# Cached sequences of layer one: other places and another order for the loads of their keys and values

## The chip, the core and the metric

The kernel runs on one core of a Trainium2 chip. A time is device microseconds (us) of one execution of the whole program on that core. Engines are named as in the profile: PE is TensorE (matrix products and transposes), PEld its weight loads, DVE is VectorE, ACT is ScalarE, POOL is GpSimd, SP is SyncE, which in this kernel only issues DMAs. Each engine runs its own list of instructions in order and waits on semaphores that the others, or landed DMAs, raise.

## The reference

One step of a two-layer trunk, for a prompt of 512 tokens and for 8 sampled sequences of 16 new tokens each, every one of them with 256 cached tokens. What matters here is layer one for the sampled sequences:

```
q, k, v, g = split(h @ w_in_a)                     # 16 heads of 64
k_all, v_all = concat(cache_k, k), concat(cache_v, v)   # 256 cached + 16 new rows
z = q @ k_all.T / 8
a = exp(log_sigmoid(z) + sum of log_sigmoid(-z) over later keys)   # stick-breaking
o = a @ v_all
y = (o * silu(g)) @ w_out_a;  x = x + gate * rmsnorm(y)
```

So each sequence reads its own 1 MB of cached keys (256 x 1024 in 32-bit floats), 1 MB of cached values, and its 16 new value rows (64 KB), which the kernel itself has written to an output shortly before. Layer two does the like with another attention.

## The kernel before

Large products (projections, the gate's columns) are made in three passes over operands split into a high and a low part; they stand at lines 1671 to 1673 and fill most of the span. All tiles lie in one arena in on-chip memory, cut into regions by hand: X, RA, RB, RC, RD, KN of 20 KB a partition each, WR of 16 and RH of 5. A name is a view of a place there, and one place has several names over time. The order of the work is written out by hand for every engine, in the blocks `sync` (SP), `gpsimd`, `scalar`, `vector` and `tensor`; nothing schedules it later.

The stretch around the change has three parts.

The pairs (from about 230 to 370 us): the prompt's attention, two heads at a time, eight pairs, PE's `pair_a`, with the gate's projection in its gaps. SP loads the gate's weights meanwhile (`gates`, L575) and, at two fixed places, `early_a` the keys of sequences 0 and 1 (`load_k`, L588). The last product of a pair is `values_a` (L1860); it reads the prompt's values in RC, which is free for other things only when the last of them is done.

The cached sequences (370 to 424 us): PE's `sample_a(s, ...)` runs once for each of the 8 sequences. Its order for sequence s is: transpose the keys of sequence s+1 (`turn_k`, 16 transposes, L1899), transpose the result of sequence s-1 (`turn_o`, L1934), transpose the weights of sequence s (L1947), scores of sequence s+1 (L1920, L1926), and last the product of weights and values of sequence s (48 small products, L1962). ACT makes the sigmoids, DVE the running products, both copy what PE has transposed. Keys come into two places `kc[0]`, `kc[1]`, values into `vc[0]`, `vc[1]`, new rows into `vnew[0]`, `vnew[1]`, by the sequence's parity.

SP's list sets when each of these loads starts. `next_k(s)` waits until the keys of sequence s-2 have been transposed (semaphore `c_k_transposed`), then issues two DMAs of 512 KB. `load_v(s)` waits until the product of sequence s-2 is done (`c_o_ready`), then issues two DMAs of 512 KB and one of 64 KB for the new rows. SP takes them strictly in turn, so a DMA that stands behind a wait can't start before that wait is over, whatever it needs itself. Before the change the list is: keys 2, keys 3, values 2, keys 4, values 3, keys 5, and so on, the middle part as a loop in which places come from registers.

The output projection (`project` with the name ya, from 428 us): its weights come in eight loads (`load(n)`, L523) through two places `wraw[0]`, `wraw[1]`. The first two are issued at about 350 us, in the pairs. ACT splits the first (`w_high`, L779) between the sequences 6 and 7.

The lines that the text speaks of:

```
def next_k(s, b):                            # before: SP
    sp.wait_ge(c_kt, s * 4 + (HEAD - 4))     # keys s-2 transposed
    load_k(s, b)
def load_v(s, b):
    sp.wait_ge(c_av, s + (HEAD - 1))         # product s-2 done
    ...                                      # two DMAs of values, one of new rows
```

Of the kernel before, what the change touches and what calls it, by code (L numbers as in the profile page):

```python
# [28 lines left out]
P = 128  # L29
D = 1024  # L30
# [3 lines left out]
NSEQ = 8  # L34
NEW = 16
# [3 lines left out]
PK = PAST // P  # L39
# [3 lines left out]
NC = 512  # L43
# [7 lines left out]
HEAD = 8  # L51
# [45 lines left out]
def build(nc, i, o):  # L97
    ctx = ExitStack()
    with ctx:
# [3 lines left out]
        def sem(name):  # L103
            return ctx.enter_context(nc.semaphore(name))
# [7 lines left out]
        def region(kb):  # L112
            a = arena[:, at[0] * KB:(at[0] + kb) * KB]
            at[0] += kb
            return a

        X, RA, RB, RC, RD, KN = (region(20) for _ in range(6))
        X_r, RA_r = (rounded[:, 20 * KB * n:20 * KB * (n + 1)] for n in range(2))
        WR, RH = region(16), region(5)
# [7 lines left out]
        def sub(r, a, n):  # L127
            return r[:, int(a * KB):int(a * KB) + n]

        def cut(r, a, /, **dims):  # L130

            names = " ".join(dims)
            return sub(r, a, math.prod(dims.values())).rearrange(f"p ({names}) -> p {names}", **dims)
# [57 lines left out]
        def halves(r, k):  # L191
            return r[:, k:k + 4, 0:SEQ].rearrange("p (k c) n -> p k c n", c=2)

        kc = [cut(WR, 8, k=PK, c=2, n=NC), halves(kT, 0)]
        vc = [halves(kT, 4), cut(KN, 0, k=PK, c=2, n=NC)]
        vnew = [sub(KN, 16, D), sub(RC, 16, D)]
        ktc = [cut(X, 8.5 * b, k=PAIRS, n=KEYS) for b in range(2)]
        qb = cut(X, 17, k=PAIRS, n=32)
        so = cut(RH, 3, b=2, n=2 * P)
        sbeta, sstay, sex = (cut(RC, 2.25 * b, g=2, n=KEYS) for b in range(3))  # L200
        sAT = cut(RH, 0, g=2, k=3, n=P)

        kcb = [cut(WR, 8 * b, k=PK, c=2, n=NC) for b in range(2)]

# [12 lines left out]
        caches = {  # L217
            "ak": i["cache_a_k"].rearrange("a s (k p) (c h) d -> (a s) p k c (h d)", p=P, c=2),
            "av": i["cache_a_v"].rearrange("a s (k p) (c h) d -> (a s) p k c (h d)", p=P, c=2),
            "bk": i["cache_b_k"].rearrange("s (k p) (a h) c d -> s p k a (h c d)", p=P, a=2),  # L220
            "bv": i["cache_b_v"].rearrange("s (k p) (c h) d -> s p k c (h d)", p=P, c=2),
        }
# [30 lines left out]
        SL = 4  # L253
        A0, YA, B0, YB = 0, 6, 8, 14
# [14 lines left out]
        tasks, task_end = [], []  # L269
# [44 lines left out]
        def batch_buffer(m):  # L314
# [12 lines left out]
        s_mu, s_macc, s_msum, s_mout, s_mdone = (sem(n) for n in (  # L327
            "mod_slot_used", "mod_first_summed", "mod_partial_read", "mod_out", "mod_read"))
# [20 lines left out]
        c_kt, c_krA, c_krV, c_q, c_z, c_sig, c_ex, c_mul, c_t, c_at, c_av, c_or, c_ot, c_od = (sem("c_" + n) for n in (  # L349
            "k_transposed", "k_read_act", "k_read_dve", "q_staged", "z_ready", "sigmoids", "scanned",  # L350
            "a_ready", "t_ready", "at_ready", "o_ready", "o_read", "o_transposed", "o_done"))
        c_k, c_v, c_vn = ([sem(f"c_{n}_in{b}") for b in range(2)] for n in ("k", "v", "vnew"))

        b_s, b_mx, b_nb, b_p, b_rc, b_c1, b_w, b_t, b_wt, b_o, b_or = (sem("b_" + n) for n in (
# [151 lines left out]
        def _(sp):  # L506
# [12 lines left out]
            def load(n):  # L519
                ci, s = divmod(n, SL)  # L520
                if n >= 2:
                    sp.wait_ge(s_wlo, n - 1)
                sp.dma_start(wraw[n % 2].rearrange("p (k n) -> p k n", k=2), piece(chunks[ci][1], chunks[ci][2], s))\  # L523
                    .then_inc(s_w[n % 2], 16)
# [61 lines left out]
            def load_k(s, b):  # L586
                for k in range(PK):
                    sp.dma_start(kc[b][:, k], caches["ak"][s, :, k]).then_inc(c_k[b], 16)  # L588

            def next_k(s, b):  # L590
                sp.wait_ge(c_kt, s * 4 + (HEAD - 4))
                load_k(s, b)

            def load_v(s, b):
                sp.wait_ge(c_av, s + (HEAD - 1))
                for k in range(PK):
                    sp.dma_start(vc[b][:, k], caches["av"][s, :, k]).then_inc(c_v[b], 16)
                sp.dma_start(vnew[b][0:NEW, :], av_rows[s]).then_inc(c_vn[b], 16)

            def early_a(p):  # L600

                if p == 2:
                    sp.wait_ge(s_mu, BATCHES)
                    load_k(0, 0)
                elif p == 6:
                    sp.wait_ge(a_z, HEAD + 8 * 4)
                    load_k(1, 1)

            gates(0, SL * YA, early_a)
            sp.wait_ge(s_glo[0], HEAD + PAIRS)  # L610
            load(SL * YA)
            load(SL * YA + 1)
            sp.wait_ge(s_stored["av"], 32)
            sp.wait_ge(a_z, HEAD + 8 * PAIRS)
            load_v(0, 0)
            sp.wait_ge(a_av, HEAD + PAIRS)
            load_v(1, 1)
            next_k(2, 0)
            with sp.Fori(1, NSEQ // 2 - 1) as it:
                for b in range(2):  # L620
                    next_k(it * 2 + (b + 1), 1 - b)
                    load_v(it * 2 + b, b)
            next_k(NSEQ - 1, 1)
            load_v(NSEQ - 2, 0)
            load_v(NSEQ - 1, 1)
            sp.wait_ge(c_z, HEAD + 2 * NSEQ)
            sp.dma_start(x[:, 0:NT, :], i["x_prompt"].rearrange("b (t p) n -> p (b t) n", p=P)).then_inc(s_xr, 16)
            sp.dma_start(x[:, NT, :], i["x_sample"].rearrange("s q n -> (s q) n")).then_inc(s_xr, 16)
# [1029 lines left out]
        def _(pe):  # L1658
# [278 lines left out]
            def sample_a(s, b, more, first=False):  # L1937
                if more:
                    turn_k(kc, turned, bank_a, read_a, c_k, PK, c_kt, s + 1)
                if not first:  # L1940
                    turn_o(s - 1, 1 - b)
                for g in range(2):
                    pe.wait_ge(c_mul, s * 2 + (HEAD + g + 1))
                    pe.wait_ge(c_at, s * 2 + (HEAD + g - 1))
                    for k in range(3):
                        w = P if k < 2 else NEW
                        last = tp(ps[4 + g][0:w, P * k:P * (k + 1)], sbeta[:, g, P * k:P * k + w], ident)  # L1947
                    last.then_inc(c_t, 1)
                if more:
                    scores_s(s + 1, ktc, 1 - b, qb, (c_krA, c_krV), c_q, c_z, c_sig, True)  # L1950
                pe.wait_ge(c_v[b], (s - b) * 16 + 32)
                pe.wait_ge(c_vn[b], (s - b) * 8 + 16)
                pe.wait_ge(c_or, s + HEAD)
                for k in range(3):
                    w = P if k < 2 else NEW
                    for g in range(2):
                        if k == 0:
                            pe.wait_ge(c_at, s * 2 + (HEAD + g + 1))
                        for j in range(4):
                            pair = slice(P * (4 * g + j), P * (4 * g + j + 1))  # L1960
                            v_ = vc[b][:, k, g, P * j:P * (j + 1)] if k < 2 else vnew[b][0:NEW, pair]
                            last = mm(ps[6][32 * j:32 * j + 32, P * g:P * (g + 1)], sAT[0:w, g, k, 32 * j:32 * j + 32], v_,  # L1962
                                      start=k == 0 and g == 0, stop=k == 2, skip_group_check=True)
                last.then_inc(c_av, 1)
# [154 lines left out]
```

## Time and profile before

| | |
|---|---|
| median of 3 runs (lowest, highest) | 928.01 us (926.48, 928.21) |
| the profiled execution, its whole time | 926.95 us |
| its span, first to last instruction | 925.2 us |
| PE busy, share of the span | 878.4 us, 95% |
| PEld, DVE, ACT, POOL | 74%, 52%, 44%, 3% |
| granted PE clock, mean | 0.994 |
| DMA, mean over the span | 150 GB/s |

The profiled execution is one run of the program; its time is 1.06 us under the median of the three. Times within the profile count from the first instruction. The granted clock is 1.00 at 2.4 GHz and 0.50 at 1.2 GHz.

### The profile page before, as it was taken

What the parts mean: (1) busy time and instruction counts of PE and PEld (TensorE: products, weight loads), DVE (VectorE), ACT (ScalarE), POOL (GpSimd) and SP (SyncE); (2) the same over time, 40 slices, a digit from 0 to 9 for tenths busy, and PEclk for the clock granted to TensorE, in tenths of its full rate; (3) what the DMA queues carried; (4) which work ended last, traced back from release to release, by engine and by line L of the source; (5) the groups of instructions that cost most, each with busy time, mean ns of one, the idle gap of its engine ahead of it and who ended that gap; (6) DMA issues with size and microseconds to landing.
All of it is one profiled execution on the core that took longest, in us unless ns stands there. A gap on an engine that the chain in (4) does not pass through costs nothing.

```text
span 925.2 us, 15133 instructions
## 1 busy us (share of the span) xinstructions
PE 878.4 (95%) x5814; PEld 683.8 (74%) x5814; DVE 477.1 (52%) x888; ACT 408.9 (44%) x891; POOL 29.8 (3%) x79
## 2 busy tenths in 40 slices
PE   5899999999999999997999799999989999998897
PEld 4677667777777778675888688888867888776685
DVE  4442334222487776567347524342376565477835
ACT  5341221212466665567245412342246666567622
POOL 0000000000000000110000000000000000022000
PEclk9999999999999999998999999999999999999999
DMA  9955645774510202795233224343211030387522
GB/s 306 369 211 217 229 157 185 288 270 144 204 48 24 92 1 95 269 322 182 72 110 114 68 70 154 97 142 120 80 69 46 23 95 2 139 305 277 187 93 114
DMA packets 72914, 138.57 MB, mean 150 GB/s; under 512 B 4368, under 2 KB 31376, under 8 KB 72720
## 3 DMA queue, kind: packets, MB, share of 16 engines
q1 hardware_dynamic: 69360, 126.60, 39.7%
q0 software_dynamic: 3200, 11.01, 3.2%
q8 instruction: 47, 0.77, 0.3%
q14 instruction: 19, 0.16, 0.1%
q10 hardware_dynamic: 288, 0.04, 0.0%
HBM read 121.38 MB, written 16.25 MB: 149 GB/s over the span
## 4 chain that ended last, share of the span: by engine, by line
PE 83%; DVE 6%; ACT 5%; issue 3%; DMA 2%; SPq 1%; ACTq 0%; DVEq 0%
PE bank L1671 20%; PE bank L1673 19%; PE bank L1672 19%; PE bank L1745 3%; PE bank L1721 2%; PE bank L1841 2%; PE bank L1995 2%; PE bank L1860 2%; PE bank L1852 2%; PE bank L2011 2%; DMA arena<-in_mod_w_a 1%; PE bank L1920 1%; PE bank L1899 1%; PE bank L2004 1%; PE bank L2052 1%
## 5 line engine op out<-in xcount | busy, mean ns | idle before, releaser
L1671 PE MATMUL bank<-w_parts,h_parts 128*128 128x512 f32 x640 | 258.0, 403 | 10.5 <-DVE h_parts L1206 6.1
L1673 PE MATMUL bank<-w_parts,h_parts 128*128 128x512 f32 x640 | 251.2, 392 | 0.0
L1672 PE MATMUL bank<-w_parts,h_parts 128*128 128x512 f32 x640 | 250.8, 392 | 0.0
L1671 PEld LDWEIGHTS bank<-w_parts,h_parts 128*128 128x128 f32 x640 | 121.1, 189 | 44.1 <-issue 15.5
L779 ACT ACTIVATE w_parts<-arena 128x1024 fp32r<-128x1024 f32 x64 | 67.4, 1054 | 179.9 <-PE bank L1673 166.6
L1200 DVE TENSOR_TENSOR w_parts<-arena,w_parts 128x1024 fp32r<-128x1024 f32 x64 | 78.2, 1223 | 129.3 <-ACT w_parts L779 128.8
L1673 PEld LDWEIGHTS bank<-w_parts,h_parts 128*128 128x128 f32 x640 | 121.0, 189 | 26.5
L1672 PEld LDWEIGHTS bank<-w_parts,h_parts 128*128 128x128 f32 x640 | 121.4, 190 | 23.1
L1671 PE MATMUL bank<-h_parts,w_parts 128*128 128x320 f32 x256 | 89.5, 350 | 1.6 <-ACT arena L896 0.9
L1673 PE MATMUL bank<-h_parts,w_parts 128*128 128x320 f32 x256 | 79.2, 309 | 0.0
L1672 PE MATMUL bank<-h_parts,w_parts 128*128 128x320 f32 x256 | 79.0, 309 | 0.0
L1385 DVE TENSOR_TENSOR_SCAN arena<-arena 128x511 f32<-128x511 f32 (+3 forms) x64 | 52.3, 817 | 26.6 <-ACT arena L906 26.6
L1671 PEld LDWEIGHTS bank<-h_parts,w_parts 128*128 128x128 f32 x256 | 48.4, 189 | 3.1 <-issue 1.7
L1672 PEld LDWEIGHTS bank<-h_parts,w_parts 128*128 128x128 f32 x256 | 48.6, 190 | 0.0
L1673 PEld LDWEIGHTS bank<-h_parts,w_parts 128*128 128x128 f32 x256 | 48.0, 188 | 0.0
L1745 PE MATMUL bank<-const,arena 128*128 128x128 f32 x280 | 41.3, 277 | 6.8 <-DVE arena L1375 2.0
L1745 PEld LDWEIGHTS bank<-const,arena 128*128 128x128 f32 x280 | 32.6, 141 | 19.0 <-issue 5.6
L905 ACT ACTIVATE arena<-bank 128x512 f32<-128x512 f32 (+3 forms) x64 | 28.4, 443 | 38.8 <-PE bank L1852 37.8
L828 ACT ACTIVATE arena<-bank 128x512 f32<-128x512 f32 x36 | 21.5, 598 | 54.1 <-PE bank L1673 53.9
L1206 DVE TENSOR_TENSOR h_parts<-arena,h_parts 128x640 fp32r<-128x640 f32 (+1 forms) x40 | 31.2, 793 | 26.6 <-ACT h_parts L784 26.5
L784 ACT ACTIVATE h_parts<-arena 128x640 fp32r<-128x640 f32 (+1 forms) x40 | 28.0, 714 | 25.2 <-PE bank L1673 14.2
L835 ACT ACTIVATE arena<-bank 128x512 f32<-128x512 f32 x21 | 12.5, 596 | 56.1 <-PE bank L1745 56.0
(170 smaller groups left out, 1183.1 us busy)
## 6 DMA issues: line engine op xcount, KB each, us to landing
arena<-in_w_in_a SPq DMA_DIRECT2D x32, 512.0 KB, 4.0
arena<-in_mod_w_b SPq DMA_DIRECT2D x12, 1024.0 KB, 6.6
arena<-in_mod_w_a SPq DMA_DIRECT2D x10, 1024.0 KB, 10.2
arena<-in_mod_w_kv SPq DMA_DIRECT2D x8, 1024.0 KB, 6.3
arena<-in_cache_a_k SPq DMA_DIRECT2D x16, 512.0 KB, 6.1
arena<-in_cache_a_v SPq DMA_DIRECT2D x16, 512.0 KB, 4.9
arena<-in_w_kv_b SPq DMA_DIRECT2D x16, 512.0 KB, 3.8
arena<-in_w_in_b SPq DMA_DIRECT2D x16, 512.0 KB, 3.9
```

The costliest lines, as they stand in the source:

```text
L779: nc.scalar.activation(whl[:, n % 2, 0, :], wraw[n % 2], ACT.Copy).then_inc(s_whi, 1)
L784: nc.scalar.activation(hhi[:, k, n], h_src[name][:, k, n], ACT.Copy).then_inc(s_hhi, 1)
L828: nc.scalar.activation(dst_of[kind][:, t, NC * (c % 2):NC * (c % 2 + 1)], ps[t][:, :], ACT.Copy).then_inc(s_pjA, 1)
L905: nc.scalar.activation(beta[:, u % 4, 0:w], ps[u % 4][:, 0:w], ACT.Sigmoid, scale=SCALE)
L1200: nc.vector.tensor_tensor(whl[:, n % 2, 1, :], wraw[n % 2], whl[:, n % 2, 0, :].bitcast(F32), ALU.subtract)\
L1206: nc.vector.tensor_tensor(hlo[:, k, n], h_src[name][:, k, n], hhi[:, k, n].bitcast(F32), ALU.subtract)\
L1385: nc.vector.tensor_tensor_scan(ex[:, u % 2, 0:w - 1][:, ::-1], st, st, 1.0, ALU.mult, ALU.bypass)\
L1671: mm(out, ah, wh, start=start, stop=False)
L1672: mm(out, ah, wl, start=False, stop=False)
L1673: return mm(out, al, wh, start=False, stop=stop)
L1721: last = mm(ps[5][32 * j:32 * j + 32, :], cT[:, 2 * s + kk, :], batch_buffer(m)[:, kk, NC * b:NC * (b + 1)], start=s == 0, stop=s == SL - ...
L1745: last = tp(ps[uses[n][1]][:, P * b:P * (b + 1)], src[:, t, P * f:P * (f + 1)], ident)
```

## The change

Sequence 0 gets two places of its own for its values, `vfirst` (4 KB each at KN 16 and RH 0), loaded in the pairs at the third step of `gates`, right behind the keys of sequence 0, under a semaphore of its own (`c_v_first_in`). `vc[0]` is therefore free at the end of the pairs, and the values of sequence 2 go there, where the values of sequence 0 went. Both places for new rows now lie in RC (RC 12 and RC 16), so the new rows of sequence 0 are loaded behind the last `values_a`. `so` and `sAT` move from RH to RC. The first output weights are loaded between product 5 and the values of sequence 7, the second ones behind the new rows of sequence 7. SP's loop is written out, and its list reads: keys s, wait for product s-2, values s (from s = 3), new rows s, then the same for s+1.

```diff
--- before.py
+++ after.py
@@ -193,12 +193,13 @@
 
         kc = [cut(WR, 8, k=PK, c=2, n=NC), halves(kT, 0)]
         vc = [halves(kT, 4), cut(KN, 0, k=PK, c=2, n=NC)]
-        vnew = [sub(KN, 16, D), sub(RC, 16, D)]
+        vfirst = [cut(r, a, c=2, n=NC) for r, a in ((KN, 16), (RH, 0))]
+        vnew = [sub(RC, 12, D), sub(RC, 16, D)]
         ktc = [cut(X, 8.5 * b, k=PAIRS, n=KEYS) for b in range(2)]
         qb = cut(X, 17, k=PAIRS, n=32)
-        so = cut(RH, 3, b=2, n=2 * P)
+        so = cut(RC, 10, b=2, n=2 * P)
         sbeta, sstay, sex = (cut(RC, 2.25 * b, g=2, n=KEYS) for b in range(3))
-        sAT = cut(RH, 0, g=2, k=3, n=P)
+        sAT = cut(RC, 7, g=2, k=3, n=P)
 
         kcb = [cut(WR, 8 * b, k=PK, c=2, n=NC) for b in range(2)]
 
@@ -349,6 +350,7 @@
         c_kt, c_krA, c_krV, c_q, c_z, c_sig, c_ex, c_mul, c_t, c_at, c_av, c_or, c_ot, c_od = (sem("c_" + n) for n in (
             "k_transposed", "k_read_act", "k_read_dve", "q_staged", "z_ready", "sigmoids", "scanned",
             "a_ready", "t_ready", "at_ready", "o_ready", "o_read", "o_transposed", "o_done"))
+        c_v0 = sem("c_v_first_in")
         c_k, c_v, c_vn = ([sem(f"c_{n}_in{b}") for b in range(2)] for n in ("k", "v", "vnew"))
 
         b_s, b_mx, b_nb, b_p, b_rc, b_c1, b_w, b_t, b_wt, b_o, b_or = (sem("b_" + n) for n in (
@@ -592,9 +594,10 @@
                 load_k(s, b)
 
             def load_v(s, b):
-                sp.wait_ge(c_av, s + (HEAD - 1))
                 for k in range(PK):
                     sp.dma_start(vc[b][:, k], caches["av"][s, :, k]).then_inc(c_v[b], 16)
+
+            def load_new(s, b):
                 sp.dma_start(vnew[b][0:NEW, :], av_rows[s]).then_inc(c_vn[b], 16)
 
             def early_a(p):
@@ -602,27 +605,31 @@
                 if p == 2:
                     sp.wait_ge(s_mu, BATCHES)
                     load_k(0, 0)
+                    sp.wait_ge(s_mdone, len(tasks))
+                    for k in range(PK):
+                        sp.dma_start(vfirst[k], caches["av"][0, :, k]).then_inc(c_v0, 16)
                 elif p == 6:
                     sp.wait_ge(a_z, HEAD + 8 * 4)
                     load_k(1, 1)
 
             gates(0, SL * YA, early_a)
             sp.wait_ge(s_glo[0], HEAD + PAIRS)
-            load(SL * YA)
-            load(SL * YA + 1)
             sp.wait_ge(s_stored["av"], 32)
             sp.wait_ge(a_z, HEAD + 8 * PAIRS)
-            load_v(0, 0)
+            load_v(2, 0)
             sp.wait_ge(a_av, HEAD + PAIRS)
+            load_new(0, 0)
             load_v(1, 1)
-            next_k(2, 0)
-            with sp.Fori(1, NSEQ // 2 - 1) as it:
-                for b in range(2):
-                    next_k(it * 2 + (b + 1), 1 - b)
-                    load_v(it * 2 + b, b)
-            next_k(NSEQ - 1, 1)
-            load_v(NSEQ - 2, 0)
-            load_v(NSEQ - 1, 1)
+            load_new(1, 1)
+            for s in range(2, NSEQ):
+                next_k(s, s % 2)
+                sp.wait_ge(c_av, s + (HEAD - 1))
+                if s == NSEQ - 1:
+                    load(SL * YA)
+                if s > 2:
+                    load_v(s, s % 2)
+                load_new(s, s % 2)
+            load(SL * YA + 1)
             sp.wait_ge(c_z, HEAD + 2 * NSEQ)
             sp.dma_start(x[:, 0:NT, :], i["x_prompt"].rearrange("b (t p) n -> p (b t) n", p=P)).then_inc(s_xr, 16)
             sp.dma_start(x[:, NT, :], i["x_sample"].rearrange("s q n -> (s q) n")).then_inc(s_xr, 16)
@@ -1948,7 +1955,10 @@
                     last.then_inc(c_t, 1)
                 if more:
                     scores_s(s + 1, ktc, 1 - b, qb, (c_krA, c_krV), c_q, c_z, c_sig, True)
-                pe.wait_ge(c_v[b], (s - b) * 16 + 32)
+                if s == 0:
+                    pe.wait_ge(c_v0, 32)
+                else:
+                    pe.wait_ge(c_v[b], (s - b) * 16 + 32 * b)
                 pe.wait_ge(c_vn[b], (s - b) * 8 + 16)
                 pe.wait_ge(c_or, s + HEAD)
                 for k in range(3):
@@ -1958,7 +1968,8 @@
                             pe.wait_ge(c_at, s * 2 + (HEAD + g + 1))
                         for j in range(4):
                             pair = slice(P * (4 * g + j), P * (4 * g + j + 1))
-                            v_ = vc[b][:, k, g, P * j:P * (j + 1)] if k < 2 else vnew[b][0:NEW, pair]
+                            old = vfirst[k % 2] if s == 0 else vc[b][:, k % 2]
+                            v_ = old[:, g, P * j:P * (j + 1)] if k < 2 else vnew[b][0:NEW, pair]
                             last = mm(ps[6][32 * j:32 * j + 32, P * g:P * (g + 1)], sAT[0:w, g, k, 32 * j:32 * j + 32], v_,
                                       start=k == 0 and g == 0, stop=k == 2, skip_group_check=True)
                 last.then_inc(c_av, 1)
```

Two pieces of SP's list follow, each before and after. The first is the start of the sequences. The names are: `in_cache_a_v` cached values, `in_cache_a_k` cached keys (128x1024 goes to the even place, 128x2x512 to the odd one), `out_av_s` the new rows. Before, from the new rows of sequence 1 on, up to the values of sequence 2:

```order
L598 DMA arena<-out_av_s 16x1024
L588 DMA arena<-in_cache_a_k 128x1024 [waits c_k_transposed]
L588 DMA arena<-in_cache_a_k 128x1024
L619 UNCONDITIONAL_BRANCH
L619 ISA
L588 ISA [waits c_k_transposed]
L588 DMA arena<-in_cache_a_k 128x2x512
L588 ISA
L588 DMA arena<-in_cache_a_k 128x2x512
L595 REGISTER_ALU
L597 ISA [waits c_o_ready]
L597 DMA arena<-in_cache_a_v 128x2x512
```

Keys 2 and keys 3 stand one behind the other, ahead of the first wait for a product. After the change, SP's list from the new rows of sequence 0 on, up to the keys of sequence 4:

```order
L601 DMA arena<-out_av_s 16x1024 [waits a_o_ready]
L598 DMA arena<-in_cache_a_v 128x1024 x2
L601 DMA arena<-out_av_s 16x1024
L590 DMA arena<-in_cache_a_k 128x1024 [waits c_k_transposed]
L590 DMA arena<-in_cache_a_k 128x1024
L601 DMA arena<-out_av_s 16x1024 [waits c_o_ready]
L590 DMA arena<-in_cache_a_k 128x2x512 [waits c_k_transposed]
L590 DMA arena<-in_cache_a_k 128x2x512
L598 DMA arena<-in_cache_a_v 128x1024 [waits c_o_ready]
L598 DMA arena<-in_cache_a_v 128x1024
L601 DMA arena<-out_av_s 16x1024
L590 DMA arena<-in_cache_a_k 128x1024 [waits c_k_transposed]
```

Keys 3 moved behind the wait for product 0, and keys 4 behind the wait for product 1 and behind the values and new rows of sequence 3. Keys 5 to 7 stand in the same way behind products 2 to 4.

The second is the end of the sequences on SP, where `in_w_out_a` are the output weights and `in_x_prompt`, `in_x_sample` the residual stream. Before:

```order
L588 DMA arena<-in_cache_a_k 128x2x512 [waits c_k_transposed]
L588 DMA arena<-in_cache_a_k 128x2x512
L597 DMA arena<-in_cache_a_v 128x2x512 [waits c_o_ready]
L597 DMA arena<-in_cache_a_v 128x2x512
L598 DMA arena<-out_av_s 16x1024
L597 DMA arena<-in_cache_a_v 128x1024 [waits c_o_ready]
L597 DMA arena<-in_cache_a_v 128x1024
L598 DMA arena<-out_av_s 16x1024
L627 DMA arena<-in_x_prompt 128x4x1024 [waits c_z_ready]
```

Keys 7, values 6, values 7 and the residual stream follow each other. After the change, from the keys of sequence 7 on:

```order
L590 DMA arena<-in_cache_a_k 128x2x512 [waits c_k_transposed]
L590 DMA arena<-in_cache_a_k 128x2x512
L525 DMA arena<-in_w_out_a 128x2x512 [waits w_low,c_o_ready]
L598 DMA arena<-in_cache_a_v 128x1024 x2
L601 DMA arena<-out_av_s 16x1024
L525 DMA arena<-in_w_out_a 128x2x512 [waits w_low]
L634 DMA arena<-in_x_prompt 128x4x1024 [waits c_z_ready]
```

One load of output weights now stands ahead of the values of sequence 7, one behind its new rows.

## Rows read from the trace of the kernel before

**Rows 1.** The page's slices: DMA's busy tenths, 40 slices of 23.1 us.

```profile
DMA  9955645774510202795233224343211030387522
```

**Rows 2.** Waits on PE from 376 to 417.2 us: total, times, longest.

```profile
PE bank L1899 <- DMA arena<-in_cache_a_k: 0.6, 1, 0.6
```

**Rows 3.** Busy time by stretch: length, engines, then granted clock, DMA share, GB/s.

```profile
376.00:382.60 6.60, 5.29 (x85) 3.42 (x83) 4.07 (x8) 4.18 (x14) 1.93 (x6) 1.00 0.98 354
389.00:395.00 6.00, 5.80 (x95) 4.24 (x92) 4.00 (x9) 3.80 (x11) 1.10 (x4) 1.00 1.00 360
424.80:425.90 1.10, 0.00 (x0) 0.00 (x0) 1.04 (x3) 0.00 (x0) 0.00 (x0) 1.00 1.01 400
```

**Rows 4.** Timeline of PE in the sequences: start, us, line, shapes, idle before.

```profile
380.99 1.65 PE L1962 MATMUL bank<-arena 128*32 128x128 f32 x48
383.22 2.00 PE L1899 MATMUL bank<-const,arena 128*128 128x128 f32 x16 [0.58 <-DMA arena<-in_cache_a_k]
...
388.96 2.00 PE L1899 MATMUL bank<-const,arena 128*128 128x128 f32 x16
...
394.93 2.00 PE L1899 MATMUL bank<-const,arena 128*128 128x128 f32 x16
...
412.88 2.00 PE L1899 MATMUL bank<-const,arena 128*128 128x128 f32 x16
...
421.06 1.76 PE L1962 MATMUL bank<-arena 128*32 128x128 f32 x48 [0.36 <-ACT arena L963]
```

**Rows 5.** Timeline of SP: start of the issue, us taken, line, what.

```profile
363.06 1.20 SPq L597 DMA_DIRECT2D arena<-in_cache_a_v  x2
...
374.41 0.84 SPq L597 DMA_DIRECT2D arena<-in_cache_a_v  x2
375.30 0.43 SPq L598 DMA_DIRECT2D arena<-out_av_s  x1
375.77 3.89 SPq L588 DMA_DIRECT2D arena<-in_cache_a_k  x4
382.84 1.27 SPq L597 DMA_DIRECT2D arena<-in_cache_a_v  x2
...
389.09 0.82 SPq L597 DMA_DIRECT2D arena<-in_cache_a_v  x2
...
392.24 0.54 SPq L588 DMA_DIRECT2D arena<-in_cache_a_k  x1
```

**Rows 6.** The chain of waits at 376 us: start, us, what.

```profile
376.23 6.94 DMA arena<-in_cache_a_k
```

**Rows 7.** Single DMA issues, begun at 374.41, 392.24, 304.10: size, us to landing.

```profile
arena<-in_cache_a_v SPq DMA_DIRECT2D x1, 512.0 KB, 3.7
...
arena<-in_cache_a_k SPq DMA_DIRECT2D x1, 512.0 KB, 6.6
...
arena<-in_cache_a_k SPq DMA_DIRECT2D x1, 512.0 KB, 5.7
```

**Rows 8.** Busy time by stretch, where PE stood still, columns as in rows 3.

```profile
32.70:35.20 2.50, 0.00 (x0) 0.02 (x1) 1.47 (x3) 0.74 (x1) 0.00 (x0) 1.00 1.09 354
524.10:527.00 2.90, 0.00 (x1) 0.00 (x0) 1.23 (x3) 2.54 (x4) 0.00 (x0) 1.00 0.00 0
528.40:531.70 3.30, 3.30 (x9) 2.54 (x8) 0.17 (x1) 0.60 (x1) 0.00 (x0) 0.50 0.89 299
```

**Rows 9.** Timeline of PE, the first products behind those two stops.

```profile
35.21 0.47 PE L1671 MATMUL bank<-w_parts,h_parts 128*128 128x512 f32 x1 [2.56 <-DVE h_parts L1206]
...
527.09 0.50 PE L1671 MATMUL bank<-w_parts,h_parts 128*128 128x512 f32 x1 [2.99 <-DVE w_parts L1200]
```

**Rows 10.** The chain of waits, one product below and one at full clock.

```profile
430.61 0.43 PE bank L1673
...
433.76 0.23 PE bank L1673
```

**Rows 11.** Timeline of ACT: the first output weights are split.

```profile
419.28 1.05 ACT L779 ACTIVATE w_parts<-arena 128x1024 fp32r<-128x1024 f32 x1
```

## The prediction, made before the changed kernel ran

> **What bounds the kernel now.** I read the page's slices first, then the stretch of the cached sequences by busy time, the waits of PE in it, and the timelines of PE and SP side by side.
>
> The slices show DMA's busy share high from slice 16 on (counted from 0), tenths 7 and 9 in the two slices that hold 370 to 416 us [rows 1]. The table by stretch says how high: from 376 to 382.6 us the share is 0.98 at 354 GB/s, and 1.00 at 360 GB/s from 389 to 395 [rows 3]. So the queue is full there. Yet PE hardly waits for it: over the sequences PE's list of waits has one wait on a load, 0.6 us, for the keys of sequence 2 [rows 2]; it ends at 383.22 after 0.58 us of idleness [rows 4]. PE is busy 5.80 of 6.00 us in a normal sequence [rows 3]. What the reader is to see: a full queue that is not a bottleneck, because its loads start early. How early is the thing the change touches.
>
> The period of a normal sequence, start of one key transpose to the next, is 394.93 - 388.96 = 5.97 us; the one whose keys were late took 388.96 - 383.22 = 5.74 from its late start [rows 4]. So a late start gives 0.23 us back within its sequence.
>
> How early do keys start? Keys 2 and 3 are issued from 375.77 in one group of four [rows 5], keys 3 well before product 0 has even begun at 380.99 [rows 4]. Keys 5 end with the issue at 392.24, which takes 6.6 us [rows 5, 7], so they land at 398.84; they are needed one period after 394.93, at 400.9. That leaves two us to spare, because SP reaches keys 5 behind product 1 and not behind product 2.
>
> **The change, part by part.**
>
> Values of sequence 0 leave the head of the queue. Before, they were issued at 363.06 [rows 5], 18 us before their product at 380.99 [rows 4]: hidden, so moving them gives nothing. Their 1 MB in the pairs, at about 242 us, meets a DMA busy share of half at most (slices 10 and 11) [rows 1]; no engine waits there on a load that I can price, cost 0, at most the few hundredths of a gate load that starts later. Values of sequence 2 take their place at 363.06, also 0.
>
> New rows 0 now stand first at 374.41, when the last pair's product is done. They are needed at 380.99. The 512 KB load issued at 374.41 took 3.7 us [rows 7]; 64 KB take no longer, so they land by 378.1: cost 0, cover 2.9 us. But they push values 1, new rows 1 and keys 2 back by one issue, 0.43 us [rows 5]. Keys 2 land at 376.23 + 6.94 = 383.17 before [rows 6] and PE waits for exactly that, so the wait grows from 0.58 to about 1.0: +0.4 us. Bounds: 0 if the short transfer is absorbed in the queue, 0.43 if not; I take 0.4, since the landing of keys 2 was the end of a full row of transfers.
>
> The new order of SP's list is the large term. Keys s+1 now stand behind the wait for product s-2, and from s = 3 behind values s and new rows s. Keys 3: after product 0, SP starts at 382.84 [rows 5], issues new rows 2, then keys 3, the second half at about 383.7. A load of that size into that place took 5.7 us in the pairs [rows 7], so it lands at 389.4; PE wants it at 388.96 + 0.4 = 389.36. Just in time: 0.
>
> Keys 4: SP restarts after product 1, at 389.09 before [rows 5] and 389.49 now, and issues values 3 (two), new rows 3, keys 4 (two). The same five DMAs in the same order, values, new rows, keys, stand in the trace, started from an idle queue at 374.41: the last landed at 383.17, 8.76 us later [rows 5, 6]. So keys 4 land at 398.25, and PE wants them at 394.93 + 0.4 = 395.33. It stops for about 2.95 us; less the 0.23 that a late start gives back, 2.7. Product 3 is then late, but product 2 was not, and the loads behind product 2 bring keys 5 at 404.2, against 404.0 at which PE now arrives: a wait of 0.2, given back. Product 3, late, releases keys 6: late by the same 2.95, net 2.7. Keys 7 are like keys 5. So only every second key load stops PE: 0.4 + 2.7 + 2.7 = 5.8 us. In short, each stop costs the length of the five loads less 6.0 us.
>
> That length is the disputed number. Below: the first 512 KB from an idle queue takes 3.7 us [rows 7], 2.4 of it not transfer if 512 KB move at 400 GB/s, the highest rate of these rows [rows 3]; the five DMAs hold 2112 KB, 5.4 us at that rate: 7.8 us, hence 2 x 1.8 and no term for keys 2, 3.5 us in all. Above: in the full queue values 3 were issued at 389.09 and keys 5 landed at 398.84, 9.75 us [rows 5, 7]: 2 x 3.7 + 0.4 = 7.8 us. I take 8.76, because that row is the same bundle from the same state of the queue.
>
> The Trainium skill, "DMA: Bandwidth & Descriptors", section "Anatomy of one DMA", fits a DMA by about 2.0 us plus bytes over 436 GB/s. Taken for the bundle as one transfer that would be an estimate of 7.0 us, two stops of 0.9, and 2.3 us in all with keys 2. The trace speaks against it: 8.76 us for the same bundle, and 354 to 360 GB/s over whole stretches with the queue full.
>
> What the stops do to the clock. PE stood still for 2.99 us before 527.09, and the granted clock in 528.40 to 531.70 is 0.50, the lower of the two levels; PE stood still for 2.56 us before 35.21 and the clock stayed at 1.00 [rows 8, 9]. My stops of 2.95 us lie close to the first. One such stretch of 3.30 us at half clock loses 3.30 x (1 - 0.23/0.43) = 1.5 us, by the spacing of one product at either level [rows 10]. Transposes and scores are on the chain right behind a late key, so all of it counts. Bounds: 0 and, for both stops, 3.1. I take one: 1.5.
>
> The output weights. The first load now starts after product 5, which by the sum ends at about 418.8; with 3.7 us it lands at 422.5. ACT splits it at 419.28 before [rows 11], now 5.8 later at 425.1: cover 2.6 us, cost 0. Behind it come values 7 and new rows 7; the four DMAs, one half-MB fewer than the bundle, take about 8.8 - 1.5 = 7.3 us from 418.8, so 426.1, and product 7 wants them at 421.06 + 5.8 = 426.9 [rows 4]: 0, with the thinnest cover of all. The second output weights are used a whole weight slot later: 0. The loop written out and the moved places add no instruction to PE, ACT or DVE: 0.
>
> Sum: 926.95 + 5.8 + 1.5 = 934.3 for the profiled execution. That execution is 1.06 under the median of the three, and the changed kernel will be told by its median too, so I forecast 928.0 + 7.3 = 935.3 us.
>
> **Rivals.**
>
> The clock holds. For it: 2.56 us did no harm [rows 9], and the stops could be shorter than 2.95. Against: 2.99 did. Time 928.0 + 5.8 = 933.8.
>
> The bundle is short, 7.8 us. For it: fewer bytes are under way at a time than before, and 400 GB/s occurs. Against: the same bundle took 8.76. Then 928.0 + 3.5 = 931.5, with stops of about 2 us and no fall of the clock. The Trainium skill's fit, "DMA: Bandwidth & Descriptors", section "Anatomy of one DMA", would make it 930.3, as an estimate.
>
> The bundle is long and the clock falls twice. For it: loads in the full queue took 9.75. Against: after each stop the queue has drained. 928.0 + 7.8 + 3.1 = 938.9.
>
> Not slower: the keys come in time. The stretch is bound by bytes, and the change takes a megabyte of values out of the full part, from 382.84 to 363.06; the queue is then emptier wherever keys stand. Price: the wait of 0.58 us goes, of which 0.23 was given back, so -0.4, 927.6. It decides at a bundle of 6.0 us; with 2.4 us that are not transfer, 2112 KB would have to move at 600 GB/s. Or the transposes of keys 4 would have to be released by something earlier than the order shows. I find neither in the rows.
>
> **How the numbers follow.** Late keys with one fall of the clock 0.50, its own range 933.0 to 937.0; clock holds 0.22; short bundle 0.14; long bundle 0.09; not slower 0.05. The range goes from the low bound over the profiled execution, 926.95 + 3.5 = 930.5, to the long bundle's 939.0. A measurement here tells 0.2%, 1.9 us, from no change. Every case but the last is beyond that: slower 0.94. The last one's 0.4 us is within it: 0.04 for the same, and 0.02 for a gain that I have no mechanism for.
>
> **What would show it.** Right: PE's waits at the key transposes of sequences 4 and 6 end with the landing of `in_cache_a_k`, near 3 us each, those of 5 and 7 near 0.2; the wait at sequence 2 is 1.0; SP issues keys 4 at about 390.8 instead of 386; DMA's share in 389 to 416 falls under 0.9, with more idle between bundles; the clock shows 0.50 behind a stop. The chain of waits passes through loads of keys for 15 to 20 us. Wrong: waits at every sequence of the same length (then the queue never drains and the length is that of the full queue); no wait at keys 4 (then the order of SP was misread); a wait at product 7 for values or new rows; or a first output load that ACT waits for.

## The result, and the profile after

The changed kernel takes 937.98 us, the median of 4 runs (936.64 to 939.23), against 928.11 of before (926.48 to 928.69): the ratio is 1.0104, with a 95% interval of 1.0087 to 1.0122. That is 9.9 us slower; 7.3 were forecast, and 938.0 lies inside the stated range. The profiled execution took 939.23 us, the slowest of the four, with a span of 937.4 us, 12.2 over the span before.

PE's timeline at the start of each key transpose, after (start, us taken, line, shapes, idle before it and what ended it); the lines answer to [rows 4]:

```profile
371.48 2.00 PE L1906 MATMUL bank<-const,arena 128*128 128x128 f32 x16
...
384.68 2.00 PE L1906 MATMUL bank<-const,arena 128*128 128x128 f32 x16 [0.62 <-DMA arena<-in_cache_a_k]
...
390.77 2.00 PE L1906 MATMUL bank<-const,arena 128*128 128x128 f32 x16 [0.28 <-DMA arena<-in_cache_a_k]
...
399.67 2.90 PE L1906 MATMUL bank<-const,arena 128*128 128x128 f32 x16 [3.09 <-DMA arena<-in_cache_a_k]
...
406.88 2.00 PE L1906 MATMUL bank<-const,arena 128*128 128x128 f32 x16
...
416.20 2.44 PE L1906 MATMUL bank<-const,arena 128*128 128x128 f32 x16 [3.27 <-DMA arena<-in_cache_a_k]
...
423.38 2.01 PE L1906 MATMUL bank<-const,arena 128*128 128x128 f32 x16
...
432.73 1.65 PE L1973 MATMUL bank<-arena 128*32 128x128 f32 x48 [1.53 <-DMA arena<-out_av_s]
```

The first row is the transpose of keys 0 (keys 1 are left out), then keys 2 to 7, and the last is product 7. PE stops for 3.09 us before keys 4 and for 3.27 before keys 6, both ended by the landing of keys; keys 5 and 7 are not waited for. The start times also show what follows a stop: keys 4 to keys 5 takes 7.21 us and keys 6 to keys 7 takes 7.18, where 5.74 was read from the late sequence of before. The transposes themselves take 2.90 and 2.44 us there, not 2.00.

The waits of PE on loads, from 369 to 445 us (total, times, longest), answer to [rows 2]:

```profile
PE bank L1906 <- DMA arena<-in_cache_a_k: 7.3, 4, 3.3
...
PE bank L1973 <- DMA arena<-out_av_s: 1.5, 1, 1.5
```

0.6 us of waiting has become 8.8. SP's timeline (start of the issue, us taken, line, what), with [rows 5] beside it, shows why:

```profile
375.83 0.35 SPq L601 DMA_DIRECT2D arena<-out_av_s  x1
376.22 0.90 SPq L598 DMA_DIRECT2D arena<-in_cache_a_v  x2
377.16 0.43 SPq L601 DMA_DIRECT2D arena<-out_av_s  x1
377.63 0.90 SPq L590 DMA_DIRECT2D arena<-in_cache_a_k  x2
...
390.55 0.81 SPq L598 DMA_DIRECT2D arena<-in_cache_a_v  x2
391.40 1.51 SPq L601 DMA_DIRECT2D arena<-out_av_s  x1
392.96 0.90 SPq L590 DMA_DIRECT2D arena<-in_cache_a_k  x2
...
407.01 0.82 SPq L598 DMA_DIRECT2D arena<-in_cache_a_v  x2
407.87 0.43 SPq L601 DMA_DIRECT2D arena<-out_av_s  x1
408.34 0.90 SPq L590 DMA_DIRECT2D arena<-in_cache_a_k  x2
```

SP goes on at 390.55, when product 1 is done, and reaches keys 4 at 392.96. And the chain of waits (start, us, what), which before had one load of keys in the sequences [rows 6], now has three:

```profile
378.10 6.54 DMA arena<-in_cache_a_k
393.42 6.20 DMA arena<-in_cache_a_k
408.80 7.35 DMA arena<-in_cache_a_k
```

Keys 4 land at 393.42 + 6.20 = 399.62, which is 9.07 us after SP went on; keys 6 at 416.15, 9.14 us after 407.01. Last, busy time by stretch (length, engines, granted clock, DMA share, GB/s):

```profile
35.40:38.60 3.20, 3.20 (x11) 2.51 (x11) 0.00 (x0) 1.46 (x3) 0.00 (x0) 0.50 1.10 348
400.60:403.90 3.30, 3.30 (x18) 3.10 (x16) 1.87 (x4) 1.19 (x3) 0.00 (x0) 0.50 1.04 338
404.00:417.00 13.00, 9.52 (x165) 6.72 (x164) 6.10 (x12) 6.29 (x21) 2.16 (x6) 1.00 0.68 242
417.70:421.00 3.30, 3.30 (x21) 2.48 (x24) 1.49 (x4) 1.66 (x5) 0.00 (x0) 0.50 1.01 335
```

Behind each of the two stops the clock is at 0.50 for about 3.3 us. DMA's share over the thirteen us between them is 0.68; over 389 to 416 us it is 0.75, where the same stretch of time before has 0.94. The queue idles (from 406 to 407 us it moves no packet) and PE waits for it, by turns.

From these starts the sequences can be booked: the shift of a row against the same row of before is 1.42 us at keys 0, then 1.46 at keys 2, 1.81 at keys 3, 4.74, 5.97, 9.31 and 10.50 at keys 4 to 7, 11.67 at product 7, and 10.80 at the first product of the output projection (438.94 against 428.14). So 9.4 us arise in the sequences. The 1.42 us ahead of them are a stretch at half clock from 35.4 to 38.6 us, behind a stop of PE that left the clock at 1.00 in the profile of before [rows 8, 9]; nothing of the change stands there. The 1.4 us that are left of the 12.2 arise behind the first output product, where the stretches at half clock stand at other places in the two profiles (528.4 us before only, 697.5 and 861.4 us after only).

### The profile page after: what moved, and what is told of

It is laid out like the page before. It is cut to its first block, busy times and chain, and to the rows that moved or that the text cites. A ratio compares the mean times of both kernels' runs of the same rounds, so it can differ in the third digit from the quotient of the medians.

```text
span 937.4 us, 15081 instructions
## 1 busy us (share of the span) xinstructions
PE 885.1 (94%) x5814; PEld 689.4 (74%) x5814; DVE 477.6 (51%) x888; ACT 409.3 (44%) x891; POOL 29.7 (3%) x79
## 4 chain that ended last, share of the span: by engine, by line
PE 83%; DVE 5%; DMA 4%; ACT 4%; issue 2%; SPq 1%; POOL 0%; DVEq 0%; ACTq 0%
PE bank L1678 19%; PE bank L1680 18%; PE bank L1679 18%; PE bank L1752 3%; PE bank L1728 2%; PE bank L1848 2%; PE bank L2006 2%; PE bank L1906 2%; DMA arena<-in_cache_a_k 2%; PE bank L1867 2%; PE bank L1859 2%; PE bank L2022 2%; PE bank L1927 1%; DMA arena<-in_mod_w_a 1%; PE bank L2063 1%
## 5 line engine op out<-in xcount | busy, mean ns | idle before, releaser
L1752 PE MATMUL bank<-const,arena 128*128 128x128 f32 x280 | 41.7, 279 | 7.5 <-DVE arena L1382 2.0
L1752 PEld LDWEIGHTS bank<-const,arena 128*128 128x128 f32 x280 | 32.9, 142 | 20.1 <-issue 6.1
L835 ACT ACTIVATE arena<-bank 128x512 f32<-128x512 f32 x36 | 21.5, 598 | 52.6 <-PE bank L1680 52.4
L1906 PE MATMUL bank<-const,arena 128*128 128x128 f32 x256 | 34.5, 286 | 8.9 <-DMA arena<-in_cache_a_k 7.3
```

What stands on the lines that cost most here:

```text
L835: nc.scalar.activation(dst_of[kind][:, t, NC * (c % 2):NC * (c % 2 + 1)], ps[t][:, :], ACT.Copy).then_inc(s_pjA, 1)
L1752: last = tp(ps[uses[n][1]][:, P * b:P * (b + 1)], src[:, t, P * f:P * (f + 1)], ident)
L1906: last = tp(bank(("k", s, c))[:, PAST * a + P * k:PAST * a + P * (k + 1)], kcs[s % 2][:, k, j // 4, P * (j % 4):P * (j % 4 + 1)], ident)
```

## The experiments

The theory (A): the keys' place in SP's list is the loss, because the load of keys s+1 now starts only when product s-2 is done, behind the values of s; to this comes the clock, which falls behind the stops. Rivals: the moved places and the early first values cost by contention (B); the output weights' loads at the end do (C).

**Keys ahead of the wait again.** The changed kernel with one edit:

```diff
             for s in range(2, NSEQ):
-                next_k(s, s % 2)
+                if s + 1 < NSEQ:
+                    next_k(s + 1, (s + 1) % 2)
                 sp.wait_ge(c_av, s + (HEAD - 1))
```

(with `next_k(2, 0)` ahead of the loop.)

> The changed kernel with one edit: keys s+1 stand ahead of the wait for product s-2 again, as before the change; places, first values, third values and output weights stay as changed. Theory A (the loss is the place of the keys in SP's list): the stops at keys 4 and 6 go, no key wait is over 0.7 us, the time is 927.5 to 929.5. Rival B (the loss is the moved places and the early first values, by contention): stays at 934 or more. Rival C (the loss is the output weights' loads at the end of the sequences): stays at 936 or more.

927.77 us against 927.58 of before, ratio 1.0003 (0.9990 to 1.0015): the whole loss is gone, with all places, first values and output weights as changed. B and C fall, as causes of the loss by themselves. Its waits of PE (369 to 445 us) have one on a load:

```profile
PE bank L1908 <- DMA arena<-in_cache_a_k: 1.0, 1, 1.0
```

This one is for keys 2 and is 1.00 us, more than the 0.7 expected at most. Up to keys 2 the list is that of the changed kernel, where the wait was 0.62; in the eight profiles told of here that have this list up to keys 2, the wait for them is 0.45 to 1.15 us, so it varies by more than the difference.

**The order alone.** The kernel before, nothing changed but SP's list (which is written out without a loop here, as it is in the run above, where that cost nothing):

```diff
-            next_k(2, 0)
-            with sp.Fori(1, NSEQ // 2 - 1) as it:
...
+            for s in range(2, NSEQ):
+                next_k(s, s % 2)
+                load_v(s, s % 2)
```

> The kernel before with the new order of SP's list alone: keys s, then wait for product s-2, values s, new rows s, written out without a loop; no place moves, no early first values, output weights in the pairs. Theory A: values 2 now stand ahead of keys 3 too, so the stops come at keys 3, 5 and 7, about 2.7 us each, 7.9 in all, and 0 to 4.5 for the clock: 935.9 to 940.4. Rivals B and C: 928, as before.

942.41 us, ratio 1.0150 (1.0120 to 1.0180): above the expected 940.4, and the stops stand where they were expected, at keys 3, 5 and 7 (PE's timeline, columns as above):

```profile
394.08 3.23 PE L1894 MATMUL bank<-const,arena 128*128 128x128 f32 x16 [3.72 <-DMA arena<-in_cache_a_k]
401.29 2.00 PE L1894 MATMUL bank<-const,arena 128*128 128x128 f32 x16
411.25 3.32 PE L1894 MATMUL bank<-const,arena 128*128 128x128 f32 x16 [3.90 <-DMA arena<-in_cache_a_k]
418.46 2.00 PE L1894 MATMUL bank<-const,arena 128*128 128x128 f32 x16
427.60 2.64 PE L1894 MATMUL bank<-const,arena 128*128 128x128 f32 x16 [3.09 <-DMA arena<-in_cache_a_k]
```

The three stops sum to 10.7 us, and the clock was 0.50 behind the first two (394.7 to 397.9 and 411.7 to 415.0 us) and fell behind the third (0.67 over 427.6 to 430.9). With 0.23 us given back at each stop and 1.45 us for each fall that is about 14.4 of the 14.8 us lost: the expected time was too low because the stops were longer than 2.95 us each.

The order makes the loss by itself, and more than the change does, so loading the third values at once and the first ones early takes some of it back: it moves the first stop from keys 3 to keys 4 and makes three stops two.

**Keys behind the wait, but first.** The changed kernel; behind the wait for product s-2 SP issues keys s+1, then the values and new rows of s.

```diff
             for s in range(2, NSEQ):
-                next_k(s, s % 2)
                 sp.wait_ge(c_av, s + (HEAD - 1))
+                if s + 1 < NSEQ:
+                    next_k(s + 1, (s + 1) % 2)
```

(with `next_k(2, 0)` ahead of the loop, here and in the next experiment.)

> The changed kernel with keys s+1 behind the wait for product s-2, but ahead of values s and new rows s. Theory A in the form 'length of what stands up to the keys, less 6.0 us': two DMAs land some 5.5 us after SP goes on, no stop over 0.3 us: 928 to 930. If the wait itself costs the time, wherever the values stand: 936 to 939.

930.46 us, ratio 1.0026 (1.0010 to 1.0041): half a microsecond over the expected 930, and 2.9 over before. The waits for keys in PE's timeline from keys 5 on:

```profile
403.42 2.00 PE L1908 MATMUL bank<-const,arena 128*128 128x128 f32 x16 [0.99 <-DMA arena<-in_cache_a_k]
409.44 2.00 PE L1908 MATMUL bank<-const,arena 128*128 128x128 f32 x16 [0.21 <-DMA arena<-in_cache_a_k]
415.72 2.00 PE L1908 MATMUL bank<-const,arena 128*128 128x128 f32 x16 [0.47 <-DMA arena<-in_cache_a_k]
```

So the wait for the product alone costs little, and the values ahead of the keys most. But 0.99 us is not under 0.3: keys 5, issued at 396.51 us, had the values of sequence 3, issued behind keys 4, still ahead of them in the queue, whose share is 0.99 from 395 to 397 us.

**One value load ahead, one behind.** The changed kernel, with the list behind the wait so:

```diff
                 if s > 2:
-                    load_v(s, s % 2)
+                    load_half(s, s % 2, 0)
                 load_new(s, s % 2)
+                if s + 1 < NSEQ:
+                    next_k(s + 1, (s + 1) % 2)
+                if s > 2:
+                    load_half(s, s % 2, 1)
```

> The changed kernel with one of the two value loads ahead of the keys and the other behind them. Theory A: the bundle up to the keys shrinks from 9.1 to about 7.6 us, stops of 1.3 to 1.6 us at keys 4 and 6, too short for the clock to fall: 931 to 933. If a stop's size does not follow the bytes ahead of the keys: 928 or 938.

935.26 us, ratio 1.0074 (1.0049 to 1.0099): a miss. PE's timeline, keys 4 to 7:

```profile
396.56 2.00 PE L1913 MATMUL bank<-const,arena 128*128 128x128 f32 x16 [1.65 <-DMA arena<-in_cache_a_k]
403.41 2.00 PE L1913 MATMUL bank<-const,arena 128*128 128x128 f32 x16 [1.03 <-DMA arena<-in_cache_a_k]
410.73 2.00 PE L1913 MATMUL bank<-const,arena 128*128 128x128 f32 x16 [1.51 <-DMA arena<-in_cache_a_k]
418.12 2.72 PE L1913 MATMUL bank<-const,arena 128*128 128x128 f32 x16 [1.58 <-DMA arena<-in_cache_a_k]
```

The first stop is near the expected size, but there are four, not two: the load put behind keys s+1 stands ahead of the next sequence's bundle. Nor were they all too short for the clock: it fell behind the last, of 1.58 us (0.66 over 418.2 to 421.3 us; the transposes took 2.72 us). By these two runs, what counts is not what the list has between the wait and the keys, but all that is still in the queue when they are issued. The order of the three is as the theory has it: 930.5, 935.3 and 938.0 with none, one and two value loads ahead.

**PE kept busy in the stops.** To separate the stops from the clock, products of no use go to PE ahead of the waits for keys 4 and 6:

```diff
+                if k_in is c_k and s in (4, 6):
+                    n = order_of.index(("k", s, 0))
+                    done(*order_of[n - 3])
+                    keep_warm(bank(("k", s, 0)), 22)
                 pe.wait_ge(k_in[s % 2], 16 * pieces * (s // 2 + 1))
```

> The changed kernel with 22 small products of no use (some 2.4 us) put on PE into its two stops, ahead of the waits for keys 4 and 6; loads and order as changed. If the falls of the clock behind the stops cost what the profile shows (keys 4 and 6 sequences 7.2 instead of 5.7 us): the clock holds at 1.00 there, these sequences take 5.7 to 6.0 us, the stops by the landing of keys stay, 935.0 to 936.0. If the clock costs nothing beyond the stops: 938, unchanged.

940.22 us, ratio 1.0117 (1.0096 to 1.0137): slower, not faster. The 22 products were too long:

```profile
395.21 5.18 PE L1673 MATMUL bank<-const 128*128 128x128 f32 x44
400.22 1.95 PE L1910 MATMUL bank<-const,arena 128*128 128x128 f32 x16
...
411.88 5.18 PE L1673 MATMUL bank<-const 128*128 128x128 f32 x44
416.90 1.94 PE L1910 MATMUL bank<-const,arena 128*128 128x128 f32 x16
```

Each is two in the trace, and after 5.2 us of them PE no longer waits for keys 4 and 6: they overran the landing. So this time decides nothing on the clock, and the run was repeated with 11, beside the changed kernel:

> As the run with the small products, but 11 of them in each stop, since 22 took 5.2 us (each counts as two in the trace) and overran the landing of the keys; 11 take 2.6 us, less than the stops of 2.9 to 3.3. If the falls of the clock cost 1.5 us at each stop: sequences 4 and 6 take 5.7 us at a clock of 1.00, stops end with the landing of the keys, and the time is 3 us under the changed kernel run beside it: 934.5 to 936. If the clock costs nothing by itself: the same as the changed kernel beside it.

> The changed kernel itself, unaltered, beside the run before on the same chip: 936.5 to 939.5, the stops at keys 4 and 6 near 3 us each, and a fall of the clock behind them in most executions.

935.82 us with 11 products (ratio 1.0069, 1.0057 to 1.0081), 938.75 without (1.0108, 1.0087 to 1.0129), on the same chip: the intervals lie apart, and the medians differ by 2.9 us. The mean granted clock of the six executions says the same: 0.987 to 0.994 with the products, 0.981 to 0.989 without. The profile with the products, busy time by stretch behind the two waits:

```profile
400.20:405.80 5.60, 5.60 (x90) 4.13 (x90) 2.59 (x6) 3.41 (x10) 0.94 (x3) 1.00 0.93 320
417.50:423.00 5.50, 5.50 (x91) 4.09 (x89) 2.53 (x5) 3.41 (x10) 0.87 (x3) 1.00 1.05 363
```

The clock is 1.00 in both, as expected. That profiled execution was the slowest of its six (938.62; the others 934.58 to 936.53) and had a new stop, 1.75 us at keys 5, behind which the clock fell too (0.54 over 407.7 to 411.0 us):

```profile
407.67 3.44 PE L1910 MATMUL bank<-const,arena 128*128 128x128 f32 x16 [1.75 <-DMA arena<-in_cache_a_k]
```

The changed kernel's own profile in this run (its second profile, below) holds the comparison within one execution:

```profile
398.76 2.91 PE L1906 MATMUL bank<-const,arena 128*128 128x128 f32 x16 [3.72 <-DMA arena<-in_cache_a_k]
405.97 2.00 PE L1906 MATMUL bank<-const,arena 128*128 128x128 f32 x16
...
415.07 2.00 PE L1906 MATMUL bank<-const,arena 128*128 128x128 f32 x16 [3.05 <-DMA arena<-in_cache_a_k]
...
421.87 2.00 PE L1906 MATMUL bank<-const,arena 128*128 128x128 f32 x16 [0.99 <-DMA arena<-in_cache_a_k]
...
429.80 2.01 PE L1973 MATMUL bank<-arena 128*32 128x128 f32 x48 [0.36 <-ACT arena L970]
```

and the granted clock behind its two stops:

```profile
399.70:402.90 3.20, 3.20 (x17) 3.11 (x16) 1.86 (x4) 1.07 (x3) 0.00 (x0) 0.50 1.03 328
415.10:420.00 4.90, 4.90 (x70) 3.77 (x74) 1.86 (x4) 2.83 (x9) 0.35 (x2) 1.00 0.99 356
```

Behind the stop of 3.72 us the clock fell and the sequence took 405.97 - 398.76 = 7.21 us; behind that of 3.05 it held and PE was done at 421.87 - 0.99 = 420.88, after 5.81. One fall costs 1.4 us. Behind these two stops the changed kernel's first profile has two falls, this one has one.

**Output weights back in the pairs.** The changed kernel with both `load` calls where they were.

```diff
             sp.wait_ge(s_glo[0], HEAD + PAIRS)
+            load(SL * YA)
+            load(SL * YA + 1)
...
-                if s == NSEQ - 1:
-                    load(SL * YA)
...
-            load(SL * YA + 1)
```

> The changed kernel with the first two output weight loads back in the pairs. The wait of 1.5 us for new rows 7 at product 7 goes, since one load less stands ahead of them. Product 7 starts 1.2 us earlier, but the end of the sequences, set by ACT, gains less: 936.8 to 937.8 against 938.0. If that wait is of the output weights' making and fully on the chain: 936.4 to 936.8. If it isn't of their making: it stays, 938.

938.81 us, ratio 1.0108 (1.0088 to 1.0127): no difference that can be measured. There is no wait for new rows at product 7 in PE's list, and product 7 waits 0.4 us for ACT as it did before the change [rows 4]:

```profile
PE bank L1905 <- DMA arena<-in_cache_a_k: 6.4, 3, 3.1
...
PE bank L1972 <- ACT arena L969: 0.4, 1, 0.4
```

But that is not shown to be this edit's doing: in the second profile of the changed kernel, with the output weights as changed, product 7 waits for ACT too (the row at 429.80 above). Of the seven profiles with that place of the output weights, three have the wait for new rows (1.53, 0.51 and 0.41 us) and four have none. So it stays open whether the edit takes the wait away, and whether it gains the 0.2 to 1.2 us expected; the clock's falls differ by more from run to run.

**The pieces that look good, together.** Keys ahead of the wait and output weights in the pairs, as above, and keys 2 issued earlier, at 373.4 us:

```diff
+            next_k(2, 0)
             sp.wait_ge(a_av, HEAD + PAIRS)
             load_new(0, 0)
```

> The changed kernel's places and early first values, keys s+1 ahead of the wait for product s-2, output weights in the pairs, and keys 2 issued ahead of the wait for the last pair's product. The wait for keys 2 (0.6 to 1.0 us) goes, nothing else waits on a load: 926.9 to 928.0 against 927.6 to 928.1 of before, at the edge of what can be measured. If keys 2 were waited for because of the queue and not of their late issue: as before, 928.

928.33 us against 928.31, ratio 0.9997 (0.9988 to 1.0006). No wait of PE on a load is left in the sequences, but the time is not under the one of before, and 0.3 us over what was expected; the 0.6 us of before are too small to show in it.

## Why the prediction was right, step by step

Direction, place and mechanism held. The order alone makes the loss, and taking the order back removes it. The size came out too small: 9.9 us on the median where 7.3 were forecast. The median lies 1.0 us above the main case's own range (933.0 to 937.0), and nearest to the rival with a long bundle and two falls of the clock, 938.9, which had a chance of 0.09; only the wide range holds it. In the profile the 9.4 us of the sequences are 5.8 for the stops at keys 4 and 6, 0.4 for keys 2 and 3, 2.9 for the clock and 0.3 for product 7.

Of the signs named ahead, the stops at keys 4 and 6, DMA's share under 0.9, the clock at 0.50 behind a stop and 20.1 us of key loads in the chain came. The waits at keys 5 and 7 (0.2 expected) and the full microsecond at keys 2 did not, and SP reached keys 4 at 392.96, not at 390.8: 1.42 of that stem from the stretch ahead of the sequences, the rest from one long issue, told of at the end. One sign of being wrong came too, the wait at product 7 for new rows.

Of the terms:

- *Keys 4 and 6, 2.7 us each:* the stops came where they were put and were 3.09 and 3.27 us, against 2.95. The bundle of five DMAs took 9.07 and 9.14 us, not 8.76. With the clock's part taken out (a period of 5.74 in place of 7.21 and 7.18), the shifts at keys 4 and 5 together are 2.93 + 1.23 - 1.47 = 2.7, at keys 6 and 7 they are 3.34 + 1.19 - 1.44 = 3.1: 5.8 where 5.4 were forecast. That near agreement is partly luck: in the second profile of the same kernel 8.8 us arise in the sequences with one fall of the clock, so that some 7.3 us are left there for the stops (of 3.72, 3.05 and, at keys 7, 0.99 us).
- *Keys 5 and 7, 0:* right in the profile of the change, since they landed before PE came; in the second profile keys 7 were 0.99 us late.
- *Keys 2, 0.4:* a wait of 0.62 and a shift of 0.04 in the profile of the change, inside my bounds of 0 to 0.43 but at the end that I did not take. Keys 2 were issued one place later and landed in 6.54 us instead of 6.94 [rows 6]. As the same wait is 0.45 to 1.15 us from profile to profile, the term stays open within that.
- *Keys 3, just in time:* late by 0.28, shift 0.35.
- *The clock, 1.5 for one fall:* this term was mis-sized. One fall costs 1.4 to 1.5 us, as worked out, but in the profile there were two, and keeping PE busy in the stops gives back 2.9 us on the median. The upper end, 3.1, was the better choice: I had one stop of 2.99 us with a fall and one of 2.56 without [rows 9], took stops of 2.95, and then counted half. The ground for that choice, a stop's length, does not hold either. The same two stops stand in the profile of the change with the same lengths, and there the clock fell behind the short one (0.50 from 35.4 to 38.6 us, above) and held behind the long one:

```profile
34.90 0.47 PE L1678 MATMUL bank<-w_parts,h_parts 128*128 128x512 f32 x1 [2.56 <-DVE h_parts L1213]
...
538.44 0.50 PE L1678 MATMUL bank<-w_parts,h_parts 128*128 128x512 f32 x1 [2.99 <-DVE w_parts L1207]
538.50:543.00 4.50, 4.50 (x20) 3.71 (x21) 1.71 (x2) 0.73 (x2) 0.00 (x0) 1.00 0.71 226
```

- *Output weights and product 7, 0 with the thinnest cover:* the weights were in time, the new rows were not. They landed so late that product 7 waited 1.53 us, since the four DMAs, from the output weights to the new rows, took longer than the 7.3 us that I had scaled from the bundle: from 423.51 to 432.73, 9.2. On the chain that is 11.67 - 10.50 = 1.17 us, of which 0.87 came back by the first output product, since ACT's work there does not wait for product 7 alone. In the second profile the new rows were in time, so this term, too, differs from one execution to the next.

The rivals: the clock holding happens, for one stop of two in the second profile of the same kernel. A short bundle, 7.8 us, was not seen in the changed kernel. The long one, 9.75, nearly was: the second profile has 9.60 us at keys 4 (389.12 to 398.72) and 8.93 at keys 6, and the order alone has 9.78 at its stop of 3.90 us (401.42 to 411.20). What I held against it, that the queue has drained after a stop, does not speak against it: in that last case no packet moved from 400.2 to 401.4 us, and the bundle took 9.78 us all the same. Why its length goes from 8.76 to 9.78 us stays open. The estimate by the Trainium skill, "DMA: Bandwidth & Descriptors", section "Anatomy of one DMA", taken for the bundle as one transfer, was 7.0 us; the trace has 9.1. The page gives that fit for DMAs on the path that GpSimd issues, and here SP issues them. The rival that wasn't slower is out: the queue did get emptier, 0.75 for 0.94, and that came with the loss and not with a gain.

## What to carry to other kernels

When one queue issues loads for several users, read each load's start from the wait that stands ahead of it in the list, not from its own condition; a load that was allowed to go early loses its lead as soon as another's wait is put in front of it. Measure the lead (landing to need, here 2 us of a 6 us period) before reordering, and count everything that is still in the queue, not only what the list has since the wait. A stop on TensorE can cost more than its length, because the clock may fall behind it, at 1.4 to 1.5 us a fall here. A stop's length did not tell whether it would: it fell behind stops of 1.58 and 1.75 us and held behind one of 3.05. So price one fall for each stop as the upper bound.

## What the runs showed of the hardware

Some single issues on SP take far longer than their like: the new rows at 391.40 took 1.51 us, the same DMA at 377.16 took 0.43. In just that stretch (391.4 to 392.9 us) the list of queues (packets, MB, share) shows one packet of another kind:

```profile
q8 instruction: 1, 0.02, 4.0%
```

That SP was fetching its own program then is a reading of these rows; no run here took the packet away. Nor does every long issue have such a packet: with one value load ahead and one behind, an issue at 418.47 us took 1.14 us without one. The long issue at 391.40 did not make the keys later here: the bundle that holds it took 9.07 us, the next one, without it, 9.14.
